# Moving the accumulating weight transfers of a four-feed-forward kernel: two layers' into attention stages, two layers' behind chunk landings

## The reference

```python
def conv_gated_ffn(x, w_up, w_gate, conv_w, conv_b, w_down):      # 0 and 1
    u = x @ w_up
    g = causal_dwconv(x @ w_gate, conv_w, conv_b)
    return (jax.nn.silu(g) * u) @ w_down
...
def swiglu(h, w_gate, w_up, w_down):                              # 2 and 3
    return (jax.nn.silu(h @ w_gate) * (h @ w_up)) @ w_down
...
x = layer_norm(DN_ALPHA * x + mix, ln_mix_g[i], ln_mix_b[i])      # first block, layer i
ffn = conv_gated_ffn(x, ffn_w_up[i], ffn_w_gate[i], ffn_conv_w[i], ffn_conv_b[i], ffn_w_down[i])
ple = jax.nn.sigmoid(x @ ple_w_gate[i]) * (p[i] @ ple_w_proj[i])
x = layer_norm(DN_ALPHA * x + ffn + ple, ln_ffn_g[i], ln_ffn_b[i])
```

## Time and profile before

| | |
|---|---|
| median of 3 runs (lowest, highest) | 2327.53 us (2322.48, 2331.33) |
| the profiled execution | 2325.07 us |
| its span in the trace | 2323.3 us |
| mean granted TensorE clock | 0.994 |
| stages of the trace, about | gate/up 0: 291 to 498; down 0: 500 to 605; query/key/value: 612 to 825; gate/up 1: 957 to 1160; down 1: 1163 to 1268; gate/up 2: 1279 to 1531; down 2: 1533 to 1638; hybrid mixer: 1650 to 1905; gate/up 3: 1958 to 2207; down 3: 2209 to 2314 |

### The profile page before, as it was taken

The page is one execution under the profiler, slowest core; times in us unless marked ns, Lnnn a source line. Parts: engine busy times, 40 slices in busy tenths (PEclk is TensorE's granted clock), DMA queues, the critical chain, the costliest instruction groups (busy, mean ns, idle before and its releaser), DMA issues.

```text
span 2323.3 us, 37239 instructions
## 1 busy us (share of the span) xinstructions
PE 2208.0 (95%) x13094; PEld 1892.2 (81%) x13094; DVE 1646.7 (71%) x2447; ACT 1197.6 (52%) x2126; POOL 712.5 (31%) x490
## 2 busy tenths in 40 slices
PE   8999999989999999999999999999999999989998
PEld 6677888878888878888887888888878768888986
DVE  7967655578753437665698888888657954788898
ACT  6655443446655554443465544356545665334465
POOL 6945434221333425343302322221111103322211
PEclk9999999999999999999999999999999999999999
DMA  6647455575555533556674356585444202455684
GB/s 212 190 146 269 143 144 139 140 199 190 177 190 206 201 111 108 136 137 140 151 232 141 96 127 144 136 240 176 178 160 162 78 19 90 119 131 134 144 260 140
DMA packets 103991, 362.26 MB, mean 156 GB/s; under 512 B 11920, under 2 KB 11920, under 8 KB 103184
## 3 DMA queue, kind: packets, MB, share of 16 engines
q1 hardware_dynamic: 69984, 242.91, 30.5%
q0 software_dynamic: 29760, 103.82, 20.6%
q10 hardware_dynamic: 4144, 14.16, 1.8%
HBM read 350.29 MB, written 105.91 MB: 196 GB/s over the span
## 4 chain that ended last, share of the span: by engine, by line
PE 61%; DVE 14%; DMA 12%; issue 5%; ACT 5%; DVEq 1%; POOL 1%; SPq 0%; ACTq 0%; POOLq 0%
DMA raw<-ws 12%; PE banks L852 6%; PE banks L854 6%; PE banks L853 6%; PE banks L1061 6%; PE banks L1063 6%; PE banks L1062 6%; PE banks L1191 2%; PE banks L885 2%; PE banks L887 2%; PE banks L886 2%; PE banks L1193 2%; PE banks L1192 2%; DVE banks L3039 2%; PE banks L1146 2%
## 5 line engine op out<-in xcount | busy, mean ns | idle before, releaser
L1744 ACT ACTIVATE wH<-raw 128x1024 fp32r<-128x1024 f32 x363 | 382.3, 1056 | 472.8 <-DMA raw<-ws 123.6
L674 POOL TENSOR_TENSOR wL<-raw,wH 128x1024 fp32r<-128x1024 f32 x110 | 281.7, 2566 | 588.4 <-ACT wH L1744 588.2
L852 PE MATMUL banks<-xH,wH 128*128 128x512 f32 (+1 forms) x1080 | 413.2, 383 | 12.8 <-DVE xL L2472 7.4
L853 PE MATMUL banks<-xL,wH 128*128 128x512 f32 (+1 forms) x1080 | 407.6, 377 | 0.0
L854 PE MATMUL banks<-xH,wL 128*128 128x512 f32 (+1 forms) x1080 | 407.4, 377 | 0.0
L852 PEld LDWEIGHTS banks<-xH,wH 128*128 128x128 f32 x1080 | 203.6, 189 | 58.5 <-DVE wL L2477 8.3
L854 PEld LDWEIGHTS banks<-xH,wL 128*128 128x128 f32 x1080 | 203.5, 188 | 37.9
L853 PEld LDWEIGHTS banks<-xL,wH 128*128 128x128 f32 x1080 | 203.7, 189 | 35.3
L741 POOL TENSOR_TENSOR wL<-raw,wH 128x1024 fp32r<-128x1024 f32 x36 | 98.8, 2744 | 170.9 <-ACT wH L1744 170.9
L1061 PE MATMUL banks<-wH,mixXH 128*128 128x512 f32 x320 | 124.9, 390 | 6.7 <-DVE mixXL L2885 6.7
L1063 PE MATMUL banks<-wL,mixXH 128*128 128x512 f32 x320 | 124.5, 389 | 0.0
(11 more groups left out here) (415 smaller groups left out, 6160.7 us busy)
## 6 DMA issues: line engine op xcount, KB each, us to landing
raw<-ws SPq DMA_DIRECT2D x327, 512.0 KB, 3.8
raw<-sums SPq DMA_DIRECT2D x88, 512.0 KB, 5.4
sums<-sums POOLq DMA_DIRECT2D x88, 256.0 KB, 4.4
sums<-ws POOLq DMA_DIRECT2D x44, 256.0 KB, 4.5
thirds<-ws POOLq DMA_DIRECT2D x44, 256.0 KB, 6.5
raw<-thirds SPq DMA_DIRECT2D x20, 512.0 KB, 3.6
shifted<-gpad SPq DMA_DIRECT2D x32, 258.0 KB, 5.0
thirds<-ws POOLq DMA_DIRECT2D x8, 1024.0 KB, 5.6
```

Source lines behind the costliest of these rows:

```text
L674: pool.tensor_tensor(wL[:, j, :], raw[:, j, :], fp(wH[:, j, :]), ALU.subtract).then_inc(low_ready, 1)
L852: pe.matmul(bank, wH[:, slot, cols], rh, start=start, stop=False)
L853: pe.matmul(bank, wH[:, slot, cols], rl, start=False, stop=False)
L1744: act.activation(high_slot(c)[:, 0:w], raw_slot(c)[:, 0:w], ACT.Copy).then_inc(high_ready, 1)
```

## The change

**Copies and sums.** The sums of weights lie in two arrays, `firsts` (the first sum, 128 x 512 for each pair) and `sums` (the odd chunk's, for each pair), so that a feed-forward takes 12 copies in place of 14 (11 MB in place of 13.75). Even chunks of the down product are loaded as two half copies: one from `ws`, one from `firsts` when the first addition has landed. That is 44 more DMAs on SP.

**Where the additions stand.** Feed-forward 1: `sums_of_step(1, n)`, 13 steps of up to four additions, each behind one split of the query/key/value chunks; its copies 12 splits earlier; feed-forward 2's copies 12 splits later. Feed-forward 3: copies beside 12 of the 14 rope items, and all 13 steps behind the last rope item, ahead of the output product's splits. Feed-forwards 0 and 2 keep theirs in the gate/up loop, with a wait put ahead of them (`round_there`, `tile_there`): POOL waits until the chunk on which DVE's next sums depend has landed (`raw_loaded`).

**Ends of the down products.** X and Y chunks come in another order; PE does all of the seventh product's blocks earlier; DVE adds the kept part (`add_kept`) earlier; at the start, DVE makes the first parts' lows ahead of the older convolution taps, and ACT does the first chunks' highs one place earlier. The next stage's four loads wait for PE's second finished block (`block_done`) and one of them for an X chunk, not for the last chunks.

```diff
+X_AT = [FT + i for i in (0, 1, 3, 4, 6, 7, 9, 12, 14, 15, 16)]
+Y_AT = [FT + i for i in (2, 2, 5, 5, 8, 8, 10, 10, 11, 11, 13)]
+HALF_COPIES = [(0, 4), (4, 8), (8, NP)]
+PAIR_COPIES = [(k, min(k + 2, NP)) for k in range(0, NP, 2)]
+COPIES = len(PAIR_COPIES) + 2 * len(HALF_COPIES)
...
-                    if i < FT:
-                        sp_e.wait_ge(sum_added, 16 * (3 * (NP * inst + i // 2) + (3 if i % 2 else 1)))
-                        sp_e.dma_start(to, sums[FT * inst + i]).then_inc(loaded(c), 16)
+                    n = NP * inst + i // 2
+                    if i < FT and i % 2 == 0:
+                        sp_e.dma_start(to[:, 0:S], ws[c, :, 0:S]).then_inc(loaded(c), 16)
+                        sp_e.wait_ge(first_added, 16 * n + 16)
+                        sp_e.dma_start(to[:, S:D], firsts[n]).then_inc(loaded(c), 16)
+                    elif i < FT:
+                        sp_e.wait_ge(second_added, 16 * n + 16)
+                        sp_e.wait_ge(fourth_added, 16 * n + 16)
+                        sp_e.dma_start(to, sums[n]).then_inc(loaded(c), 16)
...
                 if inst < 3:
+                    sp_e.wait_ge(block_done, (QT - 1) * FULL[f"down{inst}"] + 2)
                     for c in range(d0 + DOWN, d0 + DOWN + SLOTS):
-                        sp_e.wait_ge(chunk_done, d0 + DOWN - SLOTS + 1)
+                        if c % SLOTS == (d0 + X_AT[7]) % SLOTS:
+                            sp_e.wait_ge(chunk_done, d0 + X_AT[7] + 1)
...
+            def copy_base(inst, n):
+
+                d0, p0, k = CHUNK[f"down{inst}"], NP * inst, n - len(PAIR_COPIES)
+                if k < 0:
+                    a, b = PAIR_COPIES[n]
+                    pool.dma_start(sums[p0 + a:p0 + b], ws[d0 + 2 * a + 1:d0 + 2 * b:2]).then_inc(bases_copied, 16)
...
+            def sums_of_step(inst, j):
+
+                if j == 0:
+                    bases_there(inst)
+                if j < NP:
+                    first_sum(inst, j)
+                    third_sum(inst, j)
+                if 1 <= j <= NP:
+                    second_sum(inst, j - 1)
+                if j >= 2:
+                    fourth_sum(inst, j - 2)
...
+                    def tile_there(j, t=0):
+                        c = cp + 2 * j + 1
+                        pool.wait_ge(raw_loaded[c % SLOTS], t * 16 + 16 * LOADED[c])
...
+                with pool.Fori(0, count - 2) as t:
+                    round_there(1, t)
+                    second_sum(inst, 1, t)
+                    third_sum(inst, 1, t)
+                    low(cp + 8, t)
+                    first_sum(inst, 2, t)
+                    fourth_sum(inst, 1, t)
+                    low(cp + 9, t)
...
+                if inst == 1:
+                    for n in range(NP + 2):
+                        split(begun // SLOTS, begun % SLOTS)
+                        sums_of_step(1, n)
+                        begun += 1
...
+            for n in range(NP + 2):
+                sums_of_step(3, n)
             pool.wait_ge(low_ready, hi)
...
+                second_and_third(7, 0)
                 seventh(NP - 1, 0).then_inc(block_done, 1)
                 seventh(NP - 1, 1).then_inc(block_done, 1)
-                second_and_third(NP - 2, 0).then_inc(chunk_done, 1)
+                for k in (8, 9):
+                    second_and_third(k, 0)
                 second_and_third(NP - 1, 0).then_inc(block_done, 1)
-                second_and_third(NP - 2, 1)
-                second_and_third(NP - 1, 1).then_inc(chunk_done, 2)
+                second_and_third(7, 1).then_inc(chunk_done, 2)
+                for k in (8, 9, 10):
+                    second_and_third(k, 1).then_inc(chunk_done, 1)
...
+                    if last:
+                        part_lows(0)
                     if inst < 2:
                         older_taps(tmp[:, 1, :], tmp[:, 2, :], f, t, base + 1)
-                    if last:
-                        part_lows(0)
```

More of the change, by code:

```diff
@@ L106, in in_second_ring, with in_two_halves @@
     return any(0 <= c - CHUNK[f"down{i}"] < DOWN and (c - CHUNK[f"down{i}"]) // SLOTS % 2 for i in range(4))
-LOADED = [sum(in_second_ring(d) == in_second_ring(c) for d in range(c % SLOTS, c + 1, SLOTS)) for c in range(NCHUNKS)]
+def in_two_halves(c):
+    return any(0 <= c - CHUNK[f"down{i}"] < FT and (c - CHUNK[f"down{i}"]) % 2 == 0 for i in range(4))
+LOADED = [sum(2 if in_two_halves(d) else 1 for d in range(c % SLOTS, c + 1, SLOTS)
+              if in_second_ring(d) == in_second_ring(c)) for c in range(NCHUNKS)]
 QSETS = -(-CONV_W // LANES)
@@ L726, in plain_splits @@
                         low_of_last_sum(u, 2, t)
[L727 to L733, removed]
+                    tile_there(1, count - 1)
+                    first_sum(inst, count - 1)
@@ L734, in plain_splits @@
+                    fourth_sum(inst, count - 2)
+                    low_of_last_sum(u, 1, count - 1)
+                    second_sum(inst, count - 1)
+                    third_sum(inst, count - 1)
+                    for j in range(count, NP):
+                        first_sum(inst, j)
+                        fourth_sum(inst, j - 1)
                         second_sum(inst, j)
-                        fourth_sum(inst, j)
+                        third_sum(inst, j)
+                    fourth_sum(inst, NP - 1)
@@ L746, in plain_splits @@
+                bases_there(inst)
+                first_sum(inst, 0)
+                round_there(0)
                 second_sum(inst, 0)
-                low(c + 3)
+                third_sum(inst, 0)
+                low(cp + 4)
+                first_sum(inst, 1)
                 fourth_sum(inst, 0)
[L749 to L754, removed]
@@ L755, in plain_splits @@
-                for j in range(SEVENS[inst] - 1, NP):
-                    first_and_third(inst, j)
+                low(cp + 5)
+                with pool.Fori(0, count - 2) as t:
[6 more added lines that the diff above has]
+                    low(cp + 9, t)
+                round_there(count - 1)
@@ L757, in plain_splits @@
+                for j in range(count - 1, NP):
                     second_sum(inst, j)
+                    third_sum(inst, j)
+                    if j + 1 < NP:
+                        first_sum(inst, j + 1)
                     fourth_sum(inst, j)
[L760 to L771, removed]
@@ L1113, in down_product @@
                 pe.wait_ge(part_kept, 8 * inst + 4)
-                for k in range(0, NP - 3, 2):
+                for k in (0, 2, 4):
                     for x in (k, k + 1):
@@ L2912, in down @@
                         low_of_chunk(2 * p + 1)
-                    for k in (0, 2, 4, 6):
+                    for k in (0, 2, 4):
                         parts(NP + k, X_AT[k])
```

212 lines of the change are left out of this document (134 added, 78 removed).

## The result

| | before | after |
|---|---|---|
| median (lowest, highest), 4 runs each | 2329.43 us (2322.48, 2336.04) | 2373.69 us (2370.49, 2379.36) |
| ratio after/before, 95% interval | | 1.0193 (1.0156 to 1.023) |
| span in the trace | 2323.3 us | 2370.1 us |
| mean granted TensorE clock | 0.994 | 0.975 |

What follows compares the result with a forecast made beforehand. Late weight chunks, slowed by POOL's additions on shared DMA engines, delay DVE's sums and so PE. Terms -13 - 6.5 - 12 - 17 - 2 - 4 = -54.5 us gave 2271 us, range 2253 to 2301.

Steps and rivals of the forecast that it cites:

- a ring of four slots: Copies and half-copy loads on their queues: cost nothing, covered by four chunk slots; without that cover a half copy one issue late.
- The slow rival on the copies: Feed-forward 1's copies crowd on two DMA engines, 45 us each; POOL stands 134 us, 2405 us from this stage; chance 0.02.
- the gate/up terms: Gate/up 0 to 3: additions timed behind landings (0, 2) or moved out (1, 3) save 13, 6.5, 12 and 17 us.
- the ends: Ends of the down products: first two blocks finish 4.1 us earlier, normalisation under matmuls; -4 us, bounds -12.5 and +9.6.
- the attention stages: Query/key/value and behind the rope items: moved additions stay hidden, 0 us.
- starts of down 0 and 1: DVE makes the first parts' lows ahead of two taps: 1 us saved each, -2 us, bounds 0 and -3.1.
- idle time as length less PE's busy time: Gate/up windows: PE idle 15.1, 7.0, 16.2 and 18.2 us, 56.6 us in all, the time there is to gain.
- The steps of additions: POOL in attention stages: 6.5 us a step, under 7.6 us a chunk; 13 steps 84.5 us, under an 88.3 us wait.
- Pacing did not fail: Rival, gate/up 0 and 2: paced additions still meet loads, both keep their idle time; 2296 us, chance 0.15.
- DVE did not become the bound: Rival, gate/up 2 and 3: DVE's own work bounds them once landings are gone; 2300 us, chance 0.07.

Runs made afterwards that it cites:

- copies by chunk: The changed kernel with each copy of two odd chunks issued as two copies of one chunk: 2268.31 us, ratio to the kernel before 0.9737.

## Why the prediction was wrong

It failed at one step, on the copies: "lie on queues that wait for PE's chunks anyway: nothing, covered by a ring of four slots". They cost 105 us. A copy's *form* had been changed with its place, from 16 pieces on as many engines to 16 pieces on two, and the forecast gave the form no price: only a rival did, and it scaled a row of the old form (5.6 us). Nor did the cover hold. A ring of four slots covers a load that is some us late; it didn't cover 15 to 22 us, two chunk periods of 7.6 us and more.

The slow rival on the copies named the right place, and had it wrong in four ways. It had POOL standing for the copies' landing; in fact the chunk loads were held. It had a copy take 45 us, where the packets show some 20. It said that copies on different engines cost nothing; they did overlap (four pieces in flight and more), and loads were held all the same, because a load needs all its engines. And it got 0.02. The trace of before had what a better price needs: a load is 128 packets of 4 KB, 8 on each of 16 engines, and a copy's piece took 2.5 us and more. If the two take turns, that is 8 x 2.5 = 20 us a load, near the longest landings (22 us). The Trainium skill, "DMA: Bandwidth & Descriptors", section "Rules for kernel authors", says that a leading dimension under 16 confines a DMA to at most so many engines; the trace agrees, with two pieces in flight for one copy of two chunks, and four for one of four.

With the copies in another form, the sum of the other terms comes out (2268.3 measured, 2271 forecast), but in part by luck, since errors cancel: the gate/up terms brought 16 us more than forecast, the ends some 6 us less, and the attention stages cost 5. Times here are between the same matmuls of one trace of copies by chunk, against the kernel before:

| term | forecast | measured |
|---|---|---|
| gate/up 0 (paced) | -13 | -18.4, of which 2.1 are the start of down 0 |
| gate/up 1 (moved) | -6.5 | -13.2, of which 2.4 are the start of down 1 |
| gate/up 2 (paced) | -12 | -14.4 |
| gate/up 3 (moved) | -17 | -23.1 |
| starts of down 0 and 1 | -2 | -1.0 and -1.3: PE's gap of 2.78 us is 0.69 and 0.35 now (counted above), but one of 1.08 and 1.12 has come some 4 us behind it |
| ends of the down products | -4 | about +2: -4.8 where stages meet, +7.0 in new waits |
| attention stages, without the copies' form | 0 | +0.3, +1.0, +4.2, -0.1 |

The starts came out as reasoned, with DVE's low of the first chunk the next to be late. The gate/up terms were all too small; that of gate/up 2 is the least certain, 11 to 16 us by the traces that share its code. The step behind them, idle time as length less PE's busy time, gave too little: gate/up 1 got 10.8 us shorter (its start left out) where the rows had 7.0 us of idle time. In gate/up 3 PE's busy time fell too, from 230.8 us to 225.8 in the changed kernel, at the same clock of 1.00, so some of what the rows call busy was probably waiting.

The steps of additions were sized right. POOL's timeline behind the rope items of the changed kernel shows the last rope item, the first addition of the first step and of the eleventh, the last addition, and the next split:

```profile
1892.58 1.72 POOL L936 TENSOR_TENSOR nqL<-nqT,nqH 128x512 fp32r<-128x512 f32 x1 [1.36 <-ACT nqH L2451]
1894.25 0.91 POOL L750 DMA_DIRECT2D firsts<-ws  x1
...
1959.30 0.81 POOL L750 DMA_DIRECT2D firsts<-ws  x1 [1.87 <-DMA firsts<-ws]
...
1976.58 0.81 POOL L779 DMA_DIRECT2D sums<-sums  x1 [4.86 <-DMA sums<-sums]
1982.58 2.39 POOL L690 TENSOR_TENSOR wL<-raw,wH 128x1024 fp32r<-128x1024 f32 x1 [5.19 <-ACT wH L1846]
```

Ten steps took 65 us, 6.5 each, and all 13 took POOL 82 us (1894.3 to 1976.6, the last issue) where 84.5 was forecast. The output product's first split after them still waits for ACT.

Pacing did not fail, though it is no full cure: in gate/up 2 with copies by chunk PE is left with 6 us of idle time in place of 16.2, and DVE's waits for loads ahead of the two sums of the earlier trace rows are 14 us in place of 25. DVE did not become the bound: PE's idle time in the moved gate/up 3 is 0.2 us.

## What to carry to other kernels

Price a transfer by its form as it is issued, not by its bytes: ask how many DMA engines carry it, and how long one piece is. In this kernel a load spread over all engines landed only when the two that a copy held with long pieces were done. When a transfer is moved and rewritten in one edit, these are two changes with two prices. And where loads decide the time, it can pay to issue side traffic right behind the landing of the critical load: here that wait was worth 47 us, and without it the new order of issues was worse than the old one.

## What the runs showed of the hardware

- A 1 MB copy with an outer dimension of two has two pieces of 64 KB in flight, 2.4 us each, and its packets take 19 to 23 us; a 512 KB load beside it can take 14 to 22 us to land in place of 3 to 4. With the copy cut into rows of 2 KB, two to a packet, on two engines, loads land in some 6 to 7 us in the median.
- Four strings of long pieces hold a load for about as long as two (14.4 us against 15.5).
- Copies with four pieces of 4 KB in flight take longer themselves (11.5 us for 1 MB in place of 6.5), and the kernel's time doesn't show it.
- POOL's issue itself can stand: 62.3 us in four issues, with small pieces on two engines.
- PE's long idle times cost twice: of the 108 us by which four stages grew, 22 were busy time, at a granted clock of 0.93 to 0.95 over the stage (0.99 to 1.00 before).
